# One decoder layer on one core: expert slots refilled in strict order, the router slot loaded after the count, and a product of the last norm given to GpSimd

## The chip, the cores and the metric

The kernel runs on one core of one Trainium2 chip. The core has five engines that each follow their own queue of instructions and meet only through semaphores: TensorE (PE, matrix products), VectorE (DVE), ScalarE (ACT), GpSimd (POOL) and SyncE (SP, which here issues nearly all transfers). A transfer is split over 16 DMA engines. The metric is the time of the whole program on the device in microseconds (us), the median of several runs.

## The reference

The reference is one layer of a hybrid decoder on 256 tokens of 1024 columns, in float32:

```
h = x + W_o(sum_i sigmoid(G_i xn) * P_i(mixer_i(xn))),  xn = RMSNorm(x)
h = h + HierMoE(RMSNorm(h))
out = RMSNorm(h)

HierMoE: g_sel = argmax(x @ wg + bg)            # 4 groups
         top_v, top_i = top_k(e_in, 2)          # 2 of the 8 experts of the group
         for e in range(32):
             hid = silu(x @ w1[e]) * (x @ w3[e])
             out = out + combine[:, e] * (hid @ w2[e])
RMSNorm(x) = x * rsqrt(mean(x*x) + 1e-6) * g
```

The first half has three mixers (sparse attention, pooling, a short convolution). The second half has 32 experts of width 256, and their weights are most of what is read from memory: about 100 MB of the 138 MB of the program.

## The kernel before

The first half (to about 207 us of the profile) computes the mixers and `W_o`. The second half routes the tokens and runs the experts in 8 blocks of 4 experts. Each expert takes up to 32 tokens (`CAP`) in a pass, so a block fills the 128 rows of TensorE.

**The ring.** Weights of the experts come in chunks of 1 MB (`ECHUNK`, 128 partitions x 2048 floats). A block has 12 chunks (`NQ`): 8 for the first product (w1 and w3) and 4 for the second (w2). SBUF has a ring of 25 slots of that size (`SLOTS`), in which the first half keeps its own tiles too. Four blocks, 48 chunks, make a round (`NC`); the table `AT` gives the slot of each chunk of a round. Chunks 0 to 24 take slots 0 to 24. From chunk 25 on the table says which slot is refilled: chunk 25 takes slot 0, chunk 26 takes slot 2, chunk 27 slot 3, and so on. SP issues the loads in the order of the chunks. Ahead of each it waits on `expert_used`, which TensorE raises once for each chunk that it has read; `earlier(c)` is the chunk that held the slot last. Chunks 25 to 29 are single loads (L631), the later ones pairs of 2 MB (L634, and L647 in the loop of SP that loads the second round).

**The router slot.** Slot 24 holds, in the first half and during the routing, small tiles of the router: constants (`conr`), the mask, and `pcnt`, in which VectorE works out how many passes are needed (`count_passes`, L1333 to L1337, ended by `passes_done`). Chunk 24 is loaded into that slot at L627.

**The start of the experts on TensorE.** TensorE counts the tokens of each expert with two small products of ones (L1772, `count_full`), gathers the tokens of the first block in four steps k (L1810, two products each), waits for `passes_done`, loads the number of passes into a register (L1816) and enters the loop of blocks, whose first product on chunk 0 is L1834. Between the first products stand the gathers of the next tokens (L1802).

**The end.** After the last block VectorE and ScalarE compute the last norm. VectorE copies a half row of the tokens 128 to 255 from PSUM (L1412), sums its squares (L1413), multiplies it by the norm's vector `fing` (`gain`, L1408, 512 columns), makes the next product of 256 columns (L1408), adds up the means (L1417, L1421); GpSimd raises them to the power -0.5 (L737); then VectorE scales the tokens 0 to 127 (L1425), ScalarE the others (L989), and the result is written out. `fin`, `fing`, `last_squares` and `act_squares` are laid over slots 12 to 15 of the ring, whose chunks have been used by then.

The order on each engine is that of the code; no scheduler moves anything.

Of the kernel before, what the change touches and what calls it, by code (L numbers as in the profile page):

```python
# [6 lines left out]
ALU = mybir.AluOpType  # L7
# [6 lines left out]
P = 128  # L14
# [28 lines left out]
EPS = 1e-6  # L43
NEG = -1e30
SLOT = 2048
SLOTS = 25
# [30 lines left out]

AT = [*range(SLOTS), 0, *range(2, SLOTS - 1)]
CHUNK_SET = {n: (SET_A, SET_B)[i % 2] for i, n in enumerate(SPLITS)}

NQ1 = KT
NQ2 = NQT
NQ = NQ1 + NQ2
ROUND = 4
NC = ROUND * NQ
# [25 lines left out]
K_ID = 0  # L113
K_IOTA = K_ID + P

K_TRI = K_IOTA + CAP
K_ONE = K_TRI + P
K_SL = K_ONE + P
K_RK = K_SL + HEADS
K_FOLD = K_RK + PER_GROUP  # L120
K_CAP = K_FOLD + 32
K_FOLD2 = K_CAP + MAXPASS
K_CB = K_FOLD2 + RC

# [10 lines left out]
def build(nc, x, params, consts, front, projs, small, wgrp, vecs, routerw, routerb, experts, out):  # L135
    with ExitStack() as ctx:
# [45 lines left out]
        wg = router("wg", [P, 2, P])  # L182
        pcnt = router("pcnt", [P, 8 + MAXPASS])
        hidT = sb("hidT", [P, 4, KVG, 32])
# [59 lines left out]
        comb, rank = routed[:, 0], routed[:, 1]  # L244
        mask = over("mask", [P, NT, NE], "ring", in_router[0] - 8 - MAXPASS - 2 * P)[:]


        fin = over("fin", [P, NT, D], "ring", 12 * SLOT)
        fing = over("fing", [P, D], "ring", 13 * SLOT)
        last_squares = over("last_squares", [P, NT, D], "ring", 14 * SLOT)  # L250
        act_squares = over("act_squares", [P, NT, D], "ring", 15 * SLOT)
        xgT = kv[:].rearrange("p (k s) -> p k s", k=KT)
# [10 lines left out]
        first, second_of, both = [gflat[:, i * NT * RC:(i + 1) * NT * RC] for i in range(3)]  # L263
        top1, big1, top2, big2, behind, e2, weight, c1, c2, total = [vflat[:, 256 + 16 * i:256 + 16 * i + NT * ROWS] for i in range(10)]
        gexp = vflat[:, 416:432].rearrange("p (t e) -> p t e", t=NT)
        share1, share2 = [vflat[:, i * NT * NE:(i + 1) * NT * NE].rearrange("p (t e) -> p t e", t=NT) for i in range(2)]
# [17 lines left out]
        fold2 = conr[:, K_FOLD2 - K_TRI:K_FOLD2 + RC - K_TRI]  # L284
        steps_of_cap = conr[:, K_CAP - K_TRI:K_CAP + MAXPASS - K_TRI]

# [118 lines left out]
        dve_fin = sem("dve_fin")  # L405
        act_fin = sem("act_fin")
        comb_done = sem("comb_done")
        comb_in = sem("comb_in")
# [93 lines left out]
        SCATTERED = (3, 5, 6, 7, 7)  # L502


        def summed(t, qt):
# [12 lines left out]
        def _(sp):  # L518
# [106 lines left out]
            early(SLOT_XHI, SLOT_ATT)  # L625
            sp.wait_ge(passes_done, 1)
            sp.dma_start(ring[:, SLOT_ROUTER], single(SLOT_ROUTER)).then_inc(router_slot_in, 16)  # L627

            for c in range(SLOTS, SLOTS + SINGLES):
                sp.wait_ge(expert_used, GIVEN + earlier(c) + 1)  # L630
                sp.dma_start(ring[:, AT[c]], single(c)).then_inc(expert_in[AT[c] // 2] if c % 2 else single_in, 16)  # L631
            for c in range(SLOTS + SINGLES, NC - 2, 2):
                sp.wait_ge(expert_used, GIVEN + earlier(c + 1) + 1)
                sp.dma_start(slots_of(c), experts[c // NQ, c % NQ // 2]).then_inc(expert_in[AT[c] // 2], 16)  # L634
            half = ECHUNK // 2
            for c, f, sem_in in ((NC - 2, slice(0, ECHUNK), expert_in[AT[NC - 2] // 2]), (NC - 1, slice(0, half), last_half_in),
                                 (NC - 1, slice(half, ECHUNK), last_in)):
                sp.wait_ge(expert_used, GIVEN + earlier(c) + 1)
                sp.dma_start(ring[:, AT[c], f], single(c)[:, f]).then_inc(sem_in, 16)
# [3 lines left out]
            with sp.Fori(1, passes * (NB // ROUND)) as r:  # L643
                def pair(c):

                    sp.wait_ge(expert_used, r * NC + (GIVEN + max(earlier(c), earlier(c + 1)) + 1))
                    sp.dma_start(slots_of(c), rounds[bass.ds(r % (NB // ROUND), 1), c // NQ, c % NQ // 2]  # L647
                                 .rearrange("o p c -> (o p) c")).then_inc(expert_in[AT[c] // 2], 16)

                for c in range(0, SLOT_ROUTER, 2):  # L650
                    pair(c)
                for c, sem_in in ((SLOT_ROUTER, router_slot_in), (SLOTS, expert_in[0])):
                    o = c % 2 * ECHUNK
                    sp.wait_ge(expert_used, r * NC + (GIVEN + earlier(c) + 1))
                    sp.dma_start(ring[:, AT[c]], rounds[bass.ds(r % (NB // ROUND), 1), c // NQ, c % NQ // 2, :, o:o + ECHUNK]
                                 .rearrange("o p c -> (o p) c")).then_inc(sem_in, 16)
                for c in range(SLOTS + 1, NC - 2, 2):
                    pair(c)
                for c, f, sem_in in ((NC - 2, slice(0, ECHUNK), expert_in[AT[NC - 2] // 2]), (NC - 1, slice(0, half), last_half_in),
                                     (NC - 1, slice(half, ECHUNK), last_in)):  # L660
                    sp.wait_ge(expert_used, r * NC + (GIVEN + earlier(c) + 1))
                    o = c % 2 * ECHUNK
                    sp.dma_start(ring[:, AT[c], f], rounds[bass.ds(r % (NB // ROUND), 1), c // NQ, c % NQ // 2, :, o + f.start:o + f.stop]
                                 .rearrange("o p c -> (o p) c")).then_inc(sem_in, 16)
# [9 lines left out]
        def _(pool):  # L674
# [58 lines left out]
            nc.gpsimd.tensor_tensor(flat(comb), flat(share1), flat(share2), ALU.add).then_inc(comb_ready, 1)  # L733

            for t in range(NT):
                pool.wait_ge(means_done, 2 + t)
# [3 lines left out]
        def _(act):  # L740
# [245 lines left out]
            for half in range(2):  # L986
                c = slice(half * 512, (half + 1) * 512)
                act.wait_ge(gained, (1, 3)[half])
                nc.scalar.activation(fin[:, 1, c], fin[:, 1, c], ACT.Copy, scale=stat[:, 31:32]).then_inc(act_fin, 1)  # L989
# [4 lines left out]
        def _(dve):  # L994
# [409 lines left out]
            def gain(p, c, sums, squares_done):  # L1404
# [6 lines left out]
            half_row = last_squares[:, 1, 512:D]  # L1411
            step(nc.vector.tensor_copy(half_row, bank[5][:]))  # L1412
            step(nc.vector.scalar_tensor_tensor(last_squares[:, 1, 0:512], half_row, 1.0 / D, half_row, ALU.mult, ALU.mult,  # L1413
                                                accum_out=stat[:, 13:14]))
            gain(1, slice(0, 512), half_row, 3 * NT)
            gain(2, slice(512, 768), summed(1, 2), 3 * NT + 3)
# [13 lines left out]
        def _(pe):  # L1430
# [354 lines left out]
            def have_expert(bb, j, q):  # L1785
# [8 lines left out]
                else:  # L1794
                    pe.wait_ge(expert_in[AT[c] // 2], bb * 32 + 16 * (turn(c) + 2))

# [10 lines left out]
            pe.wait_ge(sel_step, 1)  # L1807
            for k in range(4):
                for t in range(NT):
                    ins = mm(bank[2 + k // 2][:, (k % 2) * P:(k % 2 + 1) * P], h[:, t, k * P:(k + 1) * P],  # L1810
                             flat(sel[:, t]), start=(t == 0), stop=(t == NT - 1))
                if k % 2:
                    ins.then_inc(xg_full, 1)

            pe.wait_ge(passes_done, 1)
            passes = pe.value_load(npass[0:1, 0:1], min_val=1, max_val=MAXPASS)  # L1816

# [217 lines left out]
```

## Time and profile before

| | us |
|---|---|
| median of 3 runs | 416.36 |
| lowest and highest run | 415.26, 416.62 |
| the profiled execution | 415.54 |
| its span in the profile | 413.7 |

| engine | busy us | share of the span |
|---|---|---|
| TensorE | 382.1 | 92% |
| VectorE | 198.4 | 48% |
| ScalarE | 149.0 | 36% |
| GpSimd | 12.2 | 3% |

The time of an execution is 1.84 us above its span in the profile; what lies around the span is not in the trace. 139.89 MB move over the 16 DMA engines, at a mean of 338 GB/s over the span. In the page's 40 slices the DMA engines are 60% or less busy in most slices between 83 and 176 us, and 98% or more in nearly all from 207 us to 403 us. Times in the rows are counted from the start of the span.

### The profile page before, as it was taken

How to read it: one execution, taken by the hardware profiler on the slowest of the kernel's cores; microseconds unless marked ns; L12 is line 12 of the kernel's file. 1: busy time of each engine (PE TensorE's matmuls, PEld its weight loads, DVE VectorE, ACT ScalarE, POOL GpSimd, SP SyncE). 2: the span in 40 equal slices, each digit the busy share in tenths (PEclk: the TensorE clock that was granted, in tenths of full speed). 3: DMA queues.
4: the chain of work that ended last, by engine and by line, in shares of the span. 5: the costliest groups of instructions: out<-in, count | busy, mean ns of one | idle time of the engine just before them, and what ended most of it. 6: DMA issues, size and time to landing. Idle time of an engine off the chain costs nothing.

```text
span 413.7 us, 7503 instructions
## 1 busy us (share of the span) xinstructions
PE 382.1 (92%) x2990; PEld 265.2 (64%) x2990; DVE 198.4 (48%) x392; ACT 149.0 (36%) x283; POOL 12.2 (3%) x34
## 2 busy tenths in 40 slices
PE   7999999999999999999989999999899998688582
PEld 5999988767777777788865555555355544245241
DVE  3838693999898775784263121212122221211215
ACT  6834451638565635442221222222222222112023
POOL 3000000300000000000011000000000000000001
PEclk9999999999999999999999999999999999879996
DMA  7999999643441587569998999999999999999982
GB/s 299 412 412 358 395 390 365 265 152 101 154 147 67 196 329 281 184 243 398 420 418 321 394 428 429 426 414 430 426 425 428 426 417 429 428 428 428 425 335 103
DMA packets 17599, 139.89 MB, mean 338 GB/s; under 512 B 2336, under 2 KB 2720, under 8 KB 5792
## 3 DMA queue, kind: packets, MB, share of 16 engines
q1 hardware_dynamic: 16704, 138.60, 83.5%
q10 hardware_dynamic: 864, 0.84, 0.6%
q8 instruction: 24, 0.39, 0.4%
q14 instruction: 7, 0.06, 0.0%
HBM read 138.38 MB, written 1.05 MB: 337 GB/s over the span
## 4 chain that ended last, share of the span: by engine, by line
PE 73%; DMA 13%; DVE 6%; SPq 4%; ACT 2%; issue 2%; POOL 0%; POOLq 0%; DVEq 0%; ACTq 0%
DMA ring<-in_experts 12%; PE bank L1834 10%; PE bank L1802 6%; PE bank L1874 6%; PE bank L1596 5%; PE bank L1598 4%; PE bank L1597 4%; PE bank L1454 4%; PE bank L1455 4%; PE bank L1456 4%; SPq L647 4%; PE bank L1886 3%; PE bank L1718 2%; PE bank L1719 2%; PE bank L1717 2%
## 5 line engine op out<-in xcount | busy, mean ns | idle before, releaser
L1834 PE MATMUL bank<-ring,kv 128*32 128x512 f32 x512 | 65.7, 619 | 10.1 <-DMA ring<-in_experts 8.9
L481 DVE TENSOR_TENSOR part<-ring,part 128x2048 fp32r<-128x2048 f32 (+1 forms) x26 | 57.8, 2231 | 17.1 <-ACT part L474 17.1
L474 ACT CAST part<-ring 128x2048 fp32r<-128x2048 f32 (+1 forms) x26 | 48.0, 1847 | 29.5 <-DMA ring<-in_front 29.4
L1802 PEld LDWEIGHTS bank<-qcur,h 128*128 128x128 f32 x256 | 31.7, 191 | 28.2 <-issue 27.3
L1376 DVE SCALAR_TENSOR_TENSOR ylo<-bank,stat,yN 128x256 fp32r<-128x256 f32 (+1 forms) x40 | 17.1, 430 | 54.1 <-ACT yN L952 34.1
L1596 PE MATMUL bank<-part,xhi 128*128 128x512 f32 x96 | 39.2, 408 | 0.0
L1802 PE MATMUL bank<-qcur,h 128*128 128x128 f32 x256 | 39.1, 289 | 0.0
L1874 PE MATMUL bank<-ring,hidT 128*32 128x256 f32 (+1 forms) x640 | 35.2, 342 | 3.9 <-DMA ring<-in_experts 3.4
L1598 PE MATMUL bank<-part,xlo 128*128 128x512 f32 x96 | 37.6, 391 | 0.0
L1597 PE MATMUL bank<-part,xhi 128*128 128x512 f32 x96 | 37.5, 391 | 0.0
L1454 PE MATMUL bank<-xhi,part 128*128 128x256 f32 x128 | 36.6, 286 | 0.5 <-DVE xlo L1021 0.5
L1455 PE MATMUL bank<-xlo,part 128*128 128x256 f32 x128 | 36.2, 283 | 0.0
L1456 PE MATMUL bank<-xhi,part 128*128 128x256 f32 x128 | 36.2, 283 | 0.0
L1834 PEld LDWEIGHTS bank<-ring,kv 128*32 128x32 f32 x512 | 13.0, 110 | 32.0 <-issue 23.6
L952 ACT ACTIVATE yN<-bank,stat 128x256 fp32r<-128x256 f32 (+1 forms) x40 | 17.2, 431 | 42.3 <-PE bank L1874 42.3
L944 ACT ACT_TABLE_LOAD x7 | 9.0, 1283 | 50.6 <-DVE stat L1366 50.6
L1886 PE MATMUL bank<-yN,cmbT 128*128 128x256 f32 (+1 forms) x80 | 23.4, 318 | 2.8 <-DVE ylo L1376 2.5
L1454 PEld LDWEIGHTS bank<-xhi,part 128*128 128x128 f32 x128 | 24.5, 192 | 1.7 <-DVE xlo L1021 0.9
L1874 PEld LDWEIGHTS bank<-ring,hidT 128*32 128x32 f32 x640 | 16.6, 109 | 13.6 <-ACT hidT L946 3.1
L1455 PEld LDWEIGHTS bank<-xlo,part 128*128 128x128 f32 x128 | 24.6, 192 | 0.0
L1456 PEld LDWEIGHTS bank<-xhi,part 128*128 128x128 f32 x128 | 24.6, 192 | 0.0
L1360 DVE TENSOR_TENSOR kv<-bank,prm 128x512 f32<-128x512 f32 x8 | 5.5, 692 | 39.7 <-PE bank L1802 39.7
(251 smaller groups left out, 586.9 us busy)
## 6 DMA issues: line engine op xcount, KB each, us to landing
ring<-in_experts SPq DMA_DIRECT2D x30, 2048.0 KB, 33.5
ring<-in_experts SPq DMA_DIRECT2D x34, 1024.0 KB, 8.4
ring<-in_front SPq DMA_DIRECT2D x28, 1024.0 KB, 5.4
ring<-in_front SPq DMA_DIRECT2D x4, 512.0 KB, 6.8
ring<-in_projs SPq DMA_DIRECT2D x4, 512.0 KB, 5.2
ring<-in_experts SPq DMA_DIRECT2D x4, 512.0 KB, 32.5
ring<-in_front SPq DMA_DIRECT2D x2, 560.0 KB, 9.4
h<-in_x SPq DMA_DIRECT2D x2, 512.0 KB, 3.8
```

The lines of the kernel that those rows point to most:

```text
L474: nc.scalar.copy(high(n, half)[:, 0:c].bitcast(F32R), raw(n, half)[:, 0:c]).then_inc(hi_done, 1)
L481: nc.vector.tensor_tensor(low(n, half)[:, 0:c].bitcast(F32R), raw(n, half)[:, 0:c], high(n, half)[:, 0:c], ALU.subtract).then_inc(split_do ...
L1454: mm(dst, whi, ahi, start=start, stop=False)
L1455: mm(dst, whi, alo, start=False, stop=False)
L1456: return mm(dst, wlo, ahi, start=False, stop=stop)
L1596: mm(bank[t][:], XH[:, kk, cols], whi[:, k], start=(kk == 0), stop=False)
L1597: mm(bank[t][:], XH[:, kk, cols], wlo[:, k], start=False, stop=False)
L1598: ins = mm(bank[t][:], XL[:, kk, cols], whi[:, k], start=False, stop=(kk == KT - 1))
L1802: ins = mm(bank[2][:, (k % 4) * P:(k % 4 + 1) * P], h[:, t, k * P:(k + 1) * P], flat(sel[:, t]), start=(t == 0), stop=(t == NT - 1))
L1834: ins = mm(bank[0][CAP * e:CAP * (e + 1)], xgT[:, q, CAP * e:CAP * (e + 1)], expert(j, q, e), start=(q == 0), stop=(q == NQ1 - 1))
L1874: ins = mm(second_out(p, slice(CAP * e, CAP * (e + 1))), hT[:, ht, CAP * e:CAP * (e + 1)], second_weights(j, p, ht, e), start=(ht == 0), s ...
L1886: mm(sum_of_piece(t, p), onehot, yN[:, place(p)].bitcast(F32R), start=False, stop=False)
```

## The change

1. `AT` becomes `[0..24, 0, 1, 2, ..., 22]`: chunk 26 takes slot 1, chunk 27 slot 2, and so on to chunk 47 in slot 22. So each chunk from 26 on waits for the use of a chunk that is one earlier in the order. The semaphore of arrival is no longer chosen by the slot but by `c % 24 // 2`, so that pairs keep one semaphore.
2. The vector of the steps of `CAP` moves from `conr` (in the router slot) to `con`, and `pcnt` from the router slot to a part of `vbd`. The load of chunk 24 waits for `count_full` in place of `passes_done`.
3. TensorE waits for `passes_done` and loads the number of passes ahead of the last of the four gather steps, not behind it.
4. The tiles of the last norm move down by one slot (11 to 14).
5. GpSimd makes the product of the half row with `fing` (512 columns) as soon as VectorE has copied the half row (`half_copied`), and VectorE no longer makes it. ScalarE waits for `half_gained` there. On GpSimd the product stands ahead of the powers.

```diff
-AT = [*range(SLOTS), 0, *range(2, SLOTS - 1)]
+AT = [*range(SLOTS), *range(ROUND * NQ - SLOTS)]
...
-        pcnt = router("pcnt", [P, 8 + MAXPASS])
...
+        pcnt = vflat[:, 432:440 + MAXPASS]
...
-        steps_of_cap = conr[:, K_CAP - K_TRI:K_CAP + MAXPASS - K_TRI]
+        steps_of_cap = con[:, K_CAP:K_CAP + MAXPASS]
...
+        def arrival(c):
+
+            return expert_in[c % SLOT_ROUTER // 2]
...
-            sp.wait_ge(passes_done, 1)
+            sp.wait_ge(count_full, 1)
             sp.dma_start(ring[:, SLOT_ROUTER], single(SLOT_ROUTER)).then_inc(router_slot_in, 16)
...
+            pool.wait_ge(vec_in, 16)
+            pool.wait_ge(half_copied, 1)
+            nc.gpsimd.tensor_tensor(fin[:, 1, 0:512], last_squares[:, 1, 512:D], fing[:, 0:512], ALU.mult).then_inc(half_gained, 1)
             for t in range(NT):
                 pool.wait_ge(means_done, 2 + t)
...
-                act.wait_ge(gained, (1, 3)[half])
+                act.wait_ge(*((half_gained, 1), (gained, 2))[half])
...
-            step(nc.vector.tensor_copy(half_row, bank[5][:]))
+            nc.vector.tensor_copy(half_row, bank[5][:]).then_inc(half_copied, 1)
+            dve.wait_ge(half_copied, 1)
             step(nc.vector.scalar_tensor_tensor(last_squares[:, 1, 0:512], half_row, 1.0 / D, half_row, ALU.mult, ALU.mult,
                                                 accum_out=stat[:, 13:14]))
-            gain(1, slice(0, 512), half_row, 3 * NT)
             gain(2, slice(512, 768), summed(1, 2), 3 * NT + 3)
...
             for k in range(4):
+                if k == 3:
+                    pe.wait_ge(passes_done, 1)
+                    passes = pe.value_load(npass[0:1, 0:1], min_val=1, max_val=MAXPASS)
                 for t in range(NT):
                     ins = mm(bank[2 + k // 2][:, (k % 2) * P:(k % 2 + 1) * P], h[:, t, k * P:(k + 1) * P],
                              flat(sel[:, t]), start=(t == 0), stop=(t == NT - 1))
                 if k % 2:
                     ins.then_inc(xg_full, 1)
-
-            pe.wait_ge(passes_done, 1)
-            passes = pe.value_load(npass[0:1, 0:1], min_val=1, max_val=MAXPASS)
```

TensorE at the start of the experts: `qcur` holds the selection of tokens, `npass` the number of passes, `kv` the gathered tokens. Before:

```order
L1772 MATMUL bank<-mask,conr 128x32 x2
L1810 MATMUL bank<-qcur,h 128x128 [waits sel_step]
L1810 MATMUL bank<-qcur,h 128x128 x7
L1816 TENSOR_LOAD npass [waits passes_done]
L1816 ISA x2
L1909 UNCONDITIONAL_BRANCH
L1909 ISA
L1795 ISA [waits xg0_done,hn_done]
L1834 MATMUL bank<-ring,kv 32x512 [waits expert_in0]
```

and now:

```order
L1782 MATMUL bank<-mask,conr 128x32 x2
L1823 MATMUL bank<-qcur,h 128x128 [waits sel_step]
L1823 MATMUL bank<-qcur,h 128x128 x5
L1821 TENSOR_LOAD npass [waits passes_done]
L1821 ISA x2
L1823 MATMUL bank<-qcur,h 128x128 x2
L1919 UNCONDITIONAL_BRANCH
L1919 ISA
L1805 ISA [waits xg0_done,hn_done]
L1844 MATMUL bank<-ring,kv 32x512 [waits expert_in0]
```

The load of the register has moved ahead of the last two products of the gather.

VectorE at the last norm, before:

```order
L1412 COPY last_squares<-bank 128x512 [waits comb_done]
L1413 SCALAR_TENSOR_TENSOR last_squares,stat<-last_squares 128x512 [waits dve_step]
L1408 TENSOR_TENSOR fin<-last_squares,fing 128x512 [waits ssq_done,comb_done,dve_step]
L1406 REGISTER_ALU
L1408 TENSOR_TENSOR fin<-bank,fing 128x256 [waits ssq_done,comb_done]
L1417 SCALAR_TENSOR_TENSOR stat<-stat 128x2
L1421 TENSOR_TENSOR stat<-stat 128x1 [waits ssq_done,means_done]
```

and now:

```order
L1422 COPY last_squares<-bank 128x512 [waits comb_done]
L1424 SCALAR_TENSOR_TENSOR last_squares,stat<-last_squares 128x512 [waits half_copied]
L1416 REGISTER_ALU [waits dve_step]
L1418 TENSOR_TENSOR fin<-bank,fing 128x256 [waits ssq_done,comb_done]
L1427 SCALAR_TENSOR_TENSOR stat<-stat 128x2
L1431 TENSOR_TENSOR stat<-stat 128x1 [waits ssq_done,means_done]
```

The product of 512 columns is gone from VectorE. GpSimd at the same place has it now, between the shares of the router and the powers of the means:

```order
L740 TENSOR_TENSOR routed<-vbd 128x64 [waits pool_step]
L744 TENSOR_TENSOR fin<-last_squares,fing 128x512 [waits half_copied,vec_in]
L747 TENSOR_TENSOR stat<-stat 128x1 [waits means_done] x2
L136 UNCONDITIONAL_BRANCH
```

Ahead of the change its last rows were L733 and the two of L737.

## Rows read from the trace of the kernel before

**Rows 1.** Late part of the chain of work: start, length, what it was.

```profile
348.27 49.81 DMA ring<-in_experts
```

**Rows 2.** Windows: stretch, length, engines' busy us (instructions), PEclk, DMA share, GB/s.

```profile
218.00:221.00 3.00, 2.70 (x24) 1.67 (x23) 0.98 (x4) 0.62 (x2) 0.32 (x1) 1.00 0.88 279
...
218.60:218.80 0.20, 0.20 (x4) 0.20 (x2) 0.00 (x0) 0.17 (x1) 0.00 (x0) 1.00 0.31 123
...
224.00:227.00 3.00, 3.00 (x34) 1.32 (x30) 1.85 (x6) 0.81 (x1) 0.00 (x0) 1.00 0.76 246
...
229.00:232.00 3.00, 2.87 (x27) 1.82 (x23) 0.48 (x1) 0.84 (x2) 0.00 (x0) 1.00 0.87 336
218.00:240.00 22.00, 21.25 (x214) 11.82 (x212) 5.88 (x16) 5.74 (x14) 0.32 (x1) 1.00 0.95 365
240.00:398.00 158.00, 140.69 (x1331) 73.38 (x1330) 32.29 (x80) 32.92 (x75) 0.00 (x0) 0.98 1.01 425
360.00:375.00 15.00, 11.85 (x105) 5.25 (x100) 1.46 (x4) 2.27 (x5) 0.00 (x0) 0.79 1.00 424
398.00:405.74 7.74, 7.08 (x100) 4.92 (x100) 3.00 (x7) 3.67 (x11) 0.00 (x0) 1.00 0.48 193
```

**Rows 3.** Timeline of SP, the loads of chunks 24, 25 and 26: start, length.

```profile
218.03 0.33 SPq L627 DMA_DIRECT2D ring<-in_experts  x1
220.43 0.33 SPq L631 DMA_DIRECT2D ring<-in_experts  x1
...
224.60 0.33 SPq L631 DMA_DIRECT2D ring<-in_experts  x1
```

**Rows 4.** Timeline of PE, the gather and the products on chunks 0 and 1.

```profile
216.95 2.05 PE L1810 MATMUL bank<-qcur,h 128*128 128x128 f32 x16
...
219.31 1.07 PE L1834 MATMUL bank<-ring,kv 128*32 128x512 f32 x8 [0.30 <-issue]
...
221.39 1.06 PE L1834 MATMUL bank<-ring,kv 128*32 128x512 f32 x8
```

**Rows 5.** PE's sequencer at L1816: duration ns min/median/max, first and last start.

```profile
L1816 PEldq TENSOR_LOAD <-npass x1: 490/490/490, 218.0 to 218.0; - x1
```

**Rows 6.** Timeline of DVE: the first step of the count of passes.

```profile
216.93 0.19 DVE L1333 TENSOR_REDUCE pcnt<-bank 128x1 f32<-128x32 f32 x1
```

**Rows 7.** Timeline of the last norm.

```profile
405.44 0.69 DVE L1413 SCALAR_TENSOR_TENSOR last_squares<-last_squares 128x512 f32<-128x512 f32 x1
...
406.17 0.69 DVE L1408 TENSOR_TENSOR fin<-last_squares,fing 128x512 f32<-128x512 f32 x1
...
406.78 0.42 DVE L1408 TENSOR_TENSOR fin<-bank,fing 128x256 f32<-128x256 f32 x1
407.12 0.15 DVE L1417 SCALAR_TENSOR_TENSOR stat<-stat 128x2 f32<-128x2 f32 x1
...
407.54 1.07 POOL L737 TENSOR_TENSOR stat<-stat 128x1 f32<-128x1 f32 x2 [189.16 <-DVE stat L1421]
...
408.64 1.34 ACT L989 ACTIVATE fin<-fin,stat 128x512 f32<-128x512 f32 x2 [2.02 <-POOL stat L737]
```

**Rows 8.** Timeline of products of GpSimd, and of VectorE beside them.

```profile
30.18 1.07 POOL L713 TENSOR_TENSOR rw<-rw,prm 128x512 f32<-128x512 f32 x1 [22.23 <-DMA rb<-in_routerb]
...
73.55 1.41 DVE L1118 TENSOR_SCALAR att<-att,coef 128x128 f32<-128x128 f32 x1
73.59 1.30 POOL L718 TENSOR_TENSOR mixlo<-mixed,mixhi 128x512 fp32r<-128x512 f32 x1
...
80.64 1.29 POOL L718 TENSOR_TENSOR mixlo<-mixed,mixhi 128x512 fp32r<-128x512 f32 x1
...
80.97 0.60 DVE L1104 SCALAR_TENSOR_TENSOR att<-conf,conr,bank 128x384 f32<-128x384 f32 x1
```

**Rows 9.** Two lines of DVE: duration ns min/median/max, first and last start.

```profile
L1118 DVE TENSOR_SCALAR att<-att,coef x16: 285/286/1410, 73.6 to 140.5; 128x128 f32<-128x128 f32 x16
...
L1117 DVE TENSOR_TENSOR coef<-coef,gts x16: 160/161/466, 73.1 to 140.3; 128x2 f32<-128x2 f32 x16
```

More of the change, by code:

```diff
@@ L44 @@
 NEG = -1e30
+NQ1 = KT
+NQ2 = NQT
+NQ = NQ1 + NQ2
+ROUND = 4
 SLOT = 2048
@@ L76 @@
 SLOT_ATT, SLOT_Q, SLOT_ROUTER = 22, 23, 24
-AT = [*range(SLOTS), 0, *range(2, SLOTS - 1)]
+AT = [*range(SLOTS), *range(ROUND * NQ - SLOTS)]
 CHUNK_SET = {n: (SET_A, SET_B)[i % 2] for i, n in enumerate(SPLITS)}
[L83 to L86, printed above, removed]
 NC = ROUND * NQ
@@ L114 @@
 K_IOTA = K_ID + P
-K_TRI = K_IOTA + CAP
+K_CAP = K_IOTA + CAP
+K_TRI = K_CAP + T // CAP
 K_ONE = K_TRI + P
@@ L120 @@
 K_FOLD = K_RK + PER_GROUP
-K_CAP = K_FOLD + 32
-K_FOLD2 = K_CAP + MAXPASS
+K_FOLD2 = K_FOLD + 32
 K_CB = K_FOLD2 + RC
@@ L244, in build @@
         comb, rank = routed[:, 0], routed[:, 1]
[L245 to L251, printed above, removed]
+        mask = over("mask", [P, NT, NE], "ring", in_router[0] - 2 * P)[:]
+        fin = over("fin", [P, NT, D], "ring", 11 * SLOT)
+        fing = over("fing", [P, D], "ring", 12 * SLOT)
+        last_squares = over("last_squares", [P, NT, D], "ring", 13 * SLOT)
+        act_squares = over("act_squares", [P, NT, D], "ring", 14 * SLOT)
         xgT = kv[:].rearrange("p (k s) -> p k s", k=KT)
@@ L406, in build @@
         act_fin = sem("act_fin")
+        half_copied = sem("half_copied")
+        half_gained = sem("half_gained")
         comb_done = sem("comb_done")
@@ L630, in _ @@
                 sp.wait_ge(expert_used, GIVEN + earlier(c) + 1)
-                sp.dma_start(ring[:, AT[c]], single(c)).then_inc(expert_in[AT[c] // 2] if c % 2 else single_in, 16)
+                sp.dma_start(ring[:, AT[c]], single(c)).then_inc(arrival(c) if c % 2 else single_in, 16)
             for c in range(SLOTS + SINGLES, NC - 2, 2):
                 sp.wait_ge(expert_used, GIVEN + earlier(c + 1) + 1)
-                sp.dma_start(slots_of(c), experts[c // NQ, c % NQ // 2]).then_inc(expert_in[AT[c] // 2], 16)
+                sp.dma_start(slots_of(c), experts[c // NQ, c % NQ // 2]).then_inc(arrival(c), 16)
             half = ECHUNK // 2
-            for c, f, sem_in in ((NC - 2, slice(0, ECHUNK), expert_in[AT[NC - 2] // 2]), (NC - 1, slice(0, half), last_half_in),
+            for c, f, sem_in in ((NC - 2, slice(0, ECHUNK), arrival(NC - 2)), (NC - 1, slice(0, half), last_half_in),
                                  (NC - 1, slice(half, ECHUNK), last_in)):
@@ L647, in pair @@
                     sp.dma_start(slots_of(c), rounds[bass.ds(r % (NB // ROUND), 1), c // NQ, c % NQ // 2]
-                                 .rearrange("o p c -> (o p) c")).then_inc(expert_in[AT[c] // 2], 16)
+                                 .rearrange("o p c -> (o p) c")).then_inc(arrival(c), 16)
                 for c in range(0, SLOT_ROUTER, 2):
                     pair(c)
-                for c, sem_in in ((SLOT_ROUTER, router_slot_in), (SLOTS, expert_in[0])):
+                for c, sem_in in ((SLOT_ROUTER, router_slot_in), (SLOTS, arrival(SLOTS))):
                     o = c % 2 * ECHUNK
@@ L658, in _ @@
                     pair(c)
-                for c, f, sem_in in ((NC - 2, slice(0, ECHUNK), expert_in[AT[NC - 2] // 2]), (NC - 1, slice(0, half), last_half_in),
+                for c, f, sem_in in ((NC - 2, slice(0, ECHUNK), arrival(NC - 2)), (NC - 1, slice(0, half), last_half_in),
                                      (NC - 1, slice(half, ECHUNK), last_in)):
@@ L1794, in have_expert @@
                 else:
-                    pe.wait_ge(expert_in[AT[c] // 2], bb * 32 + 16 * (turn(c) + 2))
+                    pe.wait_ge(arrival(c), bb * 32 + 16 * (turn(c) + 2))
             def gather(*ks):
```

## The prediction, made before any run

> **What bounds the kernel now.** I read the chain of work first, for what ends last. Its late part is one entry: a load of the ring that was issued at 348.27 and landed 49.81 us later [rows 1]. A load of 2 MB that takes 50 us to land stands in a queue, so the next view is the table of windows, for whether that queue is ever empty. From 240 to 398 us the DMA engines are busy all the time (share 1.01) at 425 GB/s, with no gap [rows 2]. So from 240 us on the end is set by bytes: the last chunk lands when all chunks ahead of it have moved, and no faster engine changes that.
>
> The bytes do not move at that rate in the 22 us ahead. From 218 to 240 us the mean is 365 GB/s [rows 2]. Against 425 that is 60 GB/s x 22 us = 1320 KB, or 3.1 us of transfer time. The windows show three holes: 218 to 221 at 279 GB/s (146 x 3 = 438 KB, 1.03 us), 224 to 227 at 246 (179 x 3 = 537 KB, 1.26 us), 229 to 232 at 336 (89 x 3 = 267 KB, 0.63 us); small shortfalls and surpluses make up the rest. As the queue never runs dry later, each us taken out of these holes brings the last chunk forward by one us. This is the most that the refills can give: 3.1 us.
>
> Whose fault are they? The timeline of SP says: chunk 24 is issued at 218.03, chunk 25 at 220.43, chunk 26 at 224.60 [rows 3]. The first hole is that of chunk 24: SP has nothing in flight any more when it may issue. The second is that of chunk 26, which waits until chunk 2 has been read.
>
> What follows the last chunk is a fixed tail of some 15 us, the second products, the combination, the last norm, and the write.
>
> **Part 1, the slots in order.** Today chunk 26 is issued behind the use of chunk 2, at 224.60. With the new table it waits for chunk 1, whose product ends at 221.39 + 1.06 = 222.45 [rows 4], so it is issued at about 222.5, 2.1 us sooner. What a late issue costs I take from the two holes themselves. The flow is down to 123 GB/s from 218.6 on [rows 2], 0.57 us behind the issue of chunk 24, and the first hole costs 1.03 us: so an issue needs about 0.57 + 1.03, some 1.5 us, before its bytes make up for an empty queue. The second hole agrees: chunk 25's bytes end at about 224.6, the issue at 224.60 plus 1.5 would cost 1.5, and 1.26 was seen. So a load costs max(0, issue + 1.5 - end of the bytes ahead). For chunk 26 that becomes 222.5 + 1.5 = 224.0 against about 224.6: nothing. The chunks behind it are each one use sooner too, some 1.7 to 2 us, and the second hole goes: -1.26 us at its site.
>
> **Part 2, chunk 24 behind the count.** The count of tokens is ready when VectorE starts on it at 216.93 [rows 6], at the latest; the number of passes only at 218.0 [rows 5]. SP issues chunk 24 at about 216.95 in place of 218.03. 216.95 + 1.5 = 218.45 is ahead of 218.6, so the first hole goes: -1.03 us at its site.
>
> **But a hole comes back between them.** Chunk 25 refills slot 0 in both versions, and waits for the use of chunk 0, which neither part moves forward. Chunk 24's 1 MB takes 1048 KB / 425 = 2.47 us, so its bytes now end at 218.6 + 2.5 = 221.1. Chunk 25 is issued at 220.43 plus the 0.15 us of part 3: 220.6 + 1.5 = 222.1, 1.0 us too late. So of 2.29 us in two holes 1.0 us returns in one, and 1.25 to 1.3 us are gained. The third hole, 0.63 us, has no cause that I can read: chunks 27 to 29 were in the queue by then. If it was a thin queue it goes too, if not it stays. Ends for the stream: a gain of 1.25 - 0.3 (the 1.5 us is rough) = 0.95 and of 1.25 + 0.63 + 0.2 = 2.1 us. I take the middle of the two cases of the third hole, 1.5 us.
>
> [...]
>
> **Part 3, the register load on TensorE.** The load starts at 218.0 and takes 0.49 us [rows 5]; the sequencer is then ahead of the array, which is still busy with the gather of 2.05 us from 216.95 [rows 4]. With the load ahead of the last step, its two products (four of the 16 instructions, 4 x 0.13 = 0.5 us) can be handed out only after about 218.8, where the array today has them behind it at 219.0. They then end at about 219.3 to 219.4, and the first product on chunk 0, today at 219.31, starts at 219.4 to 219.5. Bounds: 0 (they fit beside the branch) and 0.5 us (all of it in series); I take 0.15. Queued behind it on TensorE is everything of the experts, but only the first refills feel it, and it is in the sum above. The other consumers of the gather (VectorE's scaling of the last two steps) have until chunk 2's product at about 223.5: nothing.
>
> **Part 4, tiles of the norm one slot lower, constants in another tile.** The vector `fing` is loaded behind the same use as before, and 8 more columns in a small early load lie under the first half: nothing.
>
> **Part 5, the product on GpSimd.** Today VectorE makes the squares from 405.44 (0.69 us), the 512-column product from 406.17 (0.69), the 256-column one from 406.78, and starts on the means at 407.12; the powers start on GpSimd at 407.54, and ScalarE scales from 408.64, after which the write ends the program [rows 7]. Were that all, taking out the product would bring the means, the powers and the end forward by 406.78 - 406.17 = 0.61 us. GpSimd's product would run from 405.5 for 1.07 to 1.30 us [rows 8], done by 406.8, under the powers' 406.93.
>
> Against it stand the rows of products on GpSimd earlier. VectorE's L1118 takes 0.285 us at best, and 1.41 when it starts at 73.55 with GpSimd's product at 73.59: it ends as that product does, at 74.9 [rows 8, 9]. L1117, two elements wide with two operands in SBUF, takes 0.16 and once 0.47, at 73.1, where GpSimd was busy with the copy ahead of that product [rows 9]. But L1104, with one of its tensors in PSUM, takes 0.60 us inside GpSimd's product of 1.29 us at 80.64, and is not drawn out [rows 8]. So a VectorE instruction of the first kinds and a GpSimd product do not overlap, the later one waits. The squares (two operands in SBUF) are of that kind, the 256-column product (PSUM and SBUF) is not, the means L1417 (two operands in SBUF) are. `half_copied` frees both engines at once. Which is first no row tells; I take VectorE, as the signal is its own. Then GpSimd waits until 406.1, runs 1.07 to 1.30 us to 407.2 to 407.4, the 256-column product passes beside it, and L1417 stands until it is over: 407.2 to 407.4 in place of 407.12. Cost +0.05 to +0.3 us; I take +0.2, nearest to the row with two full operands (1.30).
>
> The Trainium skill ("SBUF — State Buffer", SBUF: two separate sides) has this as a rule that speaks against the change: VectorE and GpSimd share one pair of ports under an exclusive lock, and "whichever starts first gets the pair for the whole instruction", for VectorE with two SBUF inputs against a GpSimd operation that reads SBUF. By that rule part 5 costs 0.2 and without it it gives 0.6; the rows of L1117 and L1118 agree with it.
>
> **The sum.** Stream -1.5, norm +0.2: -1.3 us. The profiled execution took 415.54 (span 413.7 and 1.84 around it), so 414.2 of that kind; it lies 0.8 under the median of the runs, which is noise of the same size as the change. Against the median of 416.36 the forecast is 415.06, said as 415.1.
>
> **Rivals.**
> - *The hole only moves.* If the new hole before chunk 25 is as large as the old two, for instance because part 3 costs 0.5 us and the ramp of a load is nearer 2 us (1.26 + 1.03 - 1.85), the stream gains some 0.4 us and the norm takes 0.2: 416.2. For it: chunk 25's issue is the one that neither part moves. Against it: the ramp seen twice is 1.3 to 1.6 us.
> - *No exclusion at the end.* GpSimd's product runs beside the squares, the norm gives 0.6: -2.1 us, 414.3. Against it the rows of L1117.
> - *GpSimd first.* Its product runs 405.5 to 406.8, the squares behind it, everything 0.7 us later: -0.8, 415.6. It needs GpSimd to start ahead of VectorE's own signal.
> - *A lower clock in the tail (slower than before).* TensorE's granted clock has a mean of 0.79 from 360 to 375 us, where it is busy 11.85 of 15 us between waits for weights, while the tail from 398 has 1.00 with 7.08 us of busy TensorE [rows 2]. The change moves these waits by 1.5 us. If a low stretch (1.2 in place of 2.4 GHz) fell on the tail for its whole length, it would cost up to 7 us, for half of it 3.5: 416.36 - 1.3 + 3.5 = 418.6. It decides from a low stretch of 1.3 us / 0.5, 2.6 us in the tail, on. Against it: the pattern of waits moves as a whole.
> - *It doesn't do what it says.* The order shows it does; only that chunk 24 was held by something other than the number of passes could spoil part 2, and SP's issue 0.03 us after the load of that number began rules it out.
>
> **Chances.** Forecast, a net gain of 0.75 to 1.9 us: 0.60. The hole moves: 0.16. No exclusion: 0.08. GpSimd first: 0.10. Lower clock: 0.06. A measurement of this kernel tells about 0.3%, 1.25 us, from no change. In the forecast's case a good half lies beyond that (0.38 of 0.60), in that of no exclusion all, in that of GpSimd first a fifth: faster 0.48; slower by over 0.3% is the lower clock, 0.06; within 0.3% the rest, 0.46. The range from 414.0 to 416.4 leaves out the lower clock, a stream gain with all three holes closed, and little else.
>
> **What would show it.** SP's load of chunk 24 at about 217.0 and of chunk 26 about 2 us sooner; windows from 218 to 240 us at some 390 to 400 GB/s in place of 365, with one hole at about 221 to 223; the last block's waits about 1.5 us sooner. At the end GpSimd's product recorded with 1.7 to 2 us (its wait in it) or VectorE's squares with more than 0.69 us, and the means recorded with 0.5 to 0.9 us. Wrong if the refills are sooner and the last chunk is not, if the 218-to-240 mean stays at 365, or if the time from the squares to the powers shortens by 0.6 us.

## The result

| | us | runs |
|---|---|---|
| before | 415.67 median (415.24 to 416.62) | 5 |
| changed | 413.10 median (412.58 to 414.15) | 5 |
| ratio | 0.9940, 95% interval 0.9924 to 0.9955 | |

The change makes the kernel 2.5 us faster (1.9 to 3.2 by the interval), about twice the 1.3 us that was forecast, and its median lies below the range (414.0 to 416.4). The kernel before came out at 415.67 with five runs, 0.7 us under the 416.36 that the forecast was taken from; that is 0.7 of the 2.0 us between 415.1 and 413.10, and the size of the gain is the rest. A second set of five runs gave 412.75 us against 415.56 (ratio 0.9929, 0.9912 to 0.9947). The profiled execution has a span of 411.2 us against 413.7.

The windows of the changed kernel, with the columns of [rows 2]: stretch, length, busy us of PE, PEld, DVE, ACT and POOL, granted clock, DMA share, GB/s.

```profile
218.00:221.00 3.00, 2.65 (x21) 1.51 (x20) 1.14 (x4) 0.62 (x2) 0.46 (x2) 1.00 1.04 399
221.00:224.00 3.00, 3.00 (x28) 1.92 (x30) 0.02 (x1) 0.00 (x0) 0.00 (x0) 1.00 0.79 254
224.00:227.00 3.00, 3.00 (x30) 1.25 (x30) 1.84 (x6) 0.41 (x1) 0.00 (x0) 1.00 0.99 382
227.00:229.00 2.00, 2.00 (x24) 0.55 (x20) 0.40 (x1) 0.88 (x1) 0.00 (x0) 1.00 0.96 311
229.00:232.00 3.00, 2.88 (x26) 1.79 (x18) 0.48 (x1) 0.74 (x2) 0.00 (x0) 1.00 0.98 410
218.00:240.00 22.00, 21.21 (x212) 11.67 (x210) 6.04 (x16) 5.35 (x13) 0.46 (x2) 1.00 0.98 385
...
240.00:390.00 150.00, 137.46 (x1306) 73.17 (x1306) 31.80 (x79) 32.48 (x75) 0.00 (x0) 0.98 1.01 429
```

The same last stretch of the kernel before:

```profile
240.00:390.00 150.00, 135.20 (x1293) 71.14 (x1292) 31.81 (x79) 32.07 (x73) 0.00 (x0) 0.98 1.01 425
```

The first six lines are what was forecast: the holes at 218 and 224 us of [rows 2] are gone or nearly so (399 and 382 GB/s), one has come back at 221, and the mean from 218 to 240 is 385 GB/s in place of 365: 20 x 22 = 440 KB, 1.0 us. The last line is what was not: for 150 us in which the queue is never empty in either kernel, the stream runs at 429 GB/s in place of 425. That is 4 x 150 = 600 KB, another 1.4 us. Together 2.4 of the 2.5 us. TensorE starts its first product on the last chunk at 395.44 in place of 398.21 and VectorE the last squares at 402.67 in place of 405.44, both 2.77 us sooner. From the powers to the end of the span it is 6.4 us in place of 6.2, but over all traces of this case that stretch takes 6.0 to 6.6, so the difference tells nothing.

The loads of SP in the changed kernel, chunks 24, 25 and 26 (the second row groups chunks 25 and 26), and the row of chunk 26 by itself:

```profile
217.08 0.33 SPq L634 DMA_DIRECT2D ring<-in_experts  x1
220.83 2.41 SPq L638 DMA_DIRECT2D ring<-in_experts  x2
```

```profile
222.92 0.33 SPq L638 DMA_DIRECT2D ring<-in_experts  x1
```

Chunk 24 goes out 0.95 us sooner than in [rows 3], chunk 26 1.68 us sooner, chunk 25 0.40 us later. On TensorE the gather is now cut in two, and the first product on chunk 0 starts later than in [rows 4]:

```profile
217.12 1.61 PE L1823 MATMUL bank<-qcur,h 128*128 128x128 f32 x12
219.07 0.71 PE L1823 MATMUL bank<-qcur,h 128*128 128x128 f32 x4 [0.34 <-issue]
219.71 1.06 PE L1844 MATMUL bank<-ring,kv 128*32 128x512 f32 x8
```

The last norm, to be laid beside [rows 7]:

```profile
401.95 0.69 DVE L1422 COPY last_squares<-bank 128x512 f32<-128x512 f32 x1
...
402.67 0.69 DVE L1424 SCALAR_TENSOR_TENSOR last_squares<-last_squares 128x512 f32<-128x512 f32 x1
...
402.78 1.70 POOL L744 TENSOR_TENSOR fin<-last_squares,fing 128x512 f32<-128x512 f32 x1 [184.24 <-DVE last_squares L1422]
...
403.56 0.42 DVE L1418 TENSOR_TENSOR fin<-bank,fing 128x256 f32<-128x256 f32 x1 [0.19 <-ACT act_squares L982]
...
403.91 0.60 DVE L1427 SCALAR_TENSOR_TENSOR stat<-stat 128x2 f32<-128x2 f32 x1
404.54 0.23 DVE L1431 TENSOR_TENSOR stat<-stat 128x1 f32<-128x1 f32 x2
...
404.78 1.07 POOL L747 TENSOR_TENSOR stat<-stat 128x1 f32<-128x1 f32 x2 [0.29 <-DVE stat L1431]
```

VectorE starts its squares first, GpSimd's product 0.11 us behind it; that product is recorded with 1.70 us and ends at 404.48, and the means on two elements (L1427), which took 0.15 us in the kernel before, are recorded with 0.60 and end just behind it, at 404.51. From the start of the squares to the powers it is 2.11 us, against 407.54 - 405.44 = 2.10 in [rows 7]. The product has left VectorE and nothing has moved.

The granted clock of this last stretch, the eighth column, is 1.00, as it was before:

```profile
396.00:403.70 7.70, 6.53 (x96) 4.45 (x87) 3.53 (x9) 4.36 (x15) 0.92 (x1) 1.00 0.39 157
```

### The profile page after: what moved, and what is told of

It is laid out like the page before. It is cut to its first block, busy times and chain, and to the rows that moved or that the text cites. A ratio compares the mean times of both kernels' runs of the same rounds, so it can differ in the third digit from the quotient of the medians.

```text
span 411.2 us, 7504 instructions
## 1 busy us (share of the span) xinstructions
PE 381.5 (93%) x2990; PEld 265.6 (65%) x2990; DVE 198.6 (48%) x391; ACT 148.9 (36%) x283; POOL 13.8 (3%) x35
## 4 chain that ended last, share of the span: by engine, by line
PE 73%; DMA 13%; DVE 6%; SPq 3%; ACT 2%; issue 1%; POOL 0%; POOLq 0%; DVEq 0%; ACTq 0%
DMA ring<-in_experts 12%; PE bank L1844 10%; PE bank L1812 6%; PE bank L1884 6%; PE bank L1606 5%; PE bank L1607 4%; PE bank L1608 4%; PE bank L1464 4%; PE bank L1465 4%; PE bank L1466 4%; SPq L654 3%; PE bank L1896 3%; PE bank L1727 2%; PE bank L1728 2%; PE bank L1729 2%; PE bank L1568 1%
## 5 line engine op out<-in xcount | busy, mean ns | idle before, releaser
L1812 PEld LDWEIGHTS bank<-qcur,h 128*128 128x128 f32 x256 | 32.8, 196 | 28.4 <-issue 27.6
L1812 PE MATMUL bank<-qcur,h 128*128 128x128 f32 x256 | 40.1, 295 | 0.0
L1896 PEld LDWEIGHTS bank<-yN,cmbT 128*128 128x128 f32 x80 | 15.0, 188 | 13.9 <-DVE ylo L1386 11.1
```

The source lines that it names most:

```text
L1812: ins = mm(bank[2][:, (k % 4) * P:(k % 4 + 1) * P], h[:, t, k * P:(k + 1) * P], flat(sel[:, t]), start=(t == 0), stop=(t == NT - 1))
L1896: mm(sum_of_piece(t, p), onehot, yN[:, place(p)].bitcast(F32R), start=False, stop=False)
```

## The experiments

Each has five to eleven runs, made beside runs of the kernel before on the same chip. The ratio is to those runs. Their median is 415.56 us for the lines from "changed, again" to "refills one use late"; 415.79 for "ring moved 32 bytes", "ring as before", "norm's product on VectorE" and "register load behind"; and 415.71 for the other four. "Rate" is that of one trace of each, from 240 to 390 us. Up to 240 us the changed kernel, its second set, the one with the norm's product on VectorE and the one with the squares' factor from PSUM give TensorE, SP and the DMA engines the same instructions; their 218-to-240 column reads 385, 385, 376 and 384. So a difference below some 9 GB/s there (0.5 us) tells nothing from one trace.

| kernel | median us | ratio to before, 95% interval | 218 to 240 us, GB/s | rate, GB/s |
|---|---|---|---|---|
| before | 415.67 | | 365 | 425 |
| changed | 413.10 | 0.9940 (0.9924 to 0.9955) | 385 | 429 |
| changed, again | 412.75 | 0.9929 (0.9912 to 0.9947) | 385 | 429 |
| slots in order only | 412.95 | 0.9935 (0.9917 to 0.9954) | 385 | 429 |
| early chunk 24 only | 414.01 | 0.9963 (0.9950 to 0.9975) | 359 | 429 |
| refills one use late | 414.55 | 0.9976 (0.9963 to 0.9989) | 349 | 429 |
| before, ring moved 32 bytes | 414.12 | 0.9953 (0.9934 to 0.9971) | 360 | 429 |
| changed, ring as before | 414.41 | 0.9969 (0.9956 to 0.9981) | 384 | 425 |
| changed, ring at 128 | 414.19 | 0.9963 (0.9950 to 0.9976) | 381 | 426 |
| norm's product on VectorE | 413.04 | 0.9930 (0.9911 to 0.9948) | 376 | 429 |
| register load behind | 413.17 | 0.9934 (0.9915 to 0.9953) | 388 | 429 |
| squares' factor from PSUM | 412.86 | 0.9935 (0.9920 to 0.9949) | 384 | 429 |
| refill of slot 0 in halves | 413.28 | 0.9943 (0.9930 to 0.9955) | 382 | 429 |
| last three together | 412.47 | 0.9928 (0.9915 to 0.9941) | 389 | 429 |

**The parts one by one.** The first question was whether the higher rate is an accident of one execution or belongs to a part.

The changed kernel again:

> The changed kernel once more, beside the three parts. Theory A (all of the gain lies in the two holes of the transfers at 218 to 227 us, and the execution profiled of it had besides a lucky rate later on): about 1.3 us below the kernel before, and a mean of 425 GB/s from 240 to 390 us as before. Theory B (something in the change raises the rate of the whole stream): 2.5 us below, and 428 GB/s again.

Only the table of slots (against the changed kernel the edits are these, and the norm's product is back in VectorE's `gain`):

```diff
-            sp.wait_ge(count_full, 1)
+            sp.wait_ge(passes_done, 1)
             sp.dma_start(ring[:, SLOT_ROUTER], single(SLOT_ROUTER)).then_inc(router_slot_in, 16)
...
-            nc.gpsimd.tensor_tensor(fin[:, 1, 0:512], last_squares[:, 1, 512:D], fing[:, 0:512], ALU.mult).then_inc(half_gained, 1)
...
-                if k == 3:
-                    pe.wait_ge(passes_done, 1)
-                    passes = pe.value_load(npass[0:1, 0:1], min_val=1, max_val=MAXPASS)
```

> Only the table of slots in order (with the tiles of the norm one slot lower); chunk 24 waits for the number of passes, the register load stands behind the gather, and VectorE makes the product of the last norm. A: the hole ahead of chunk 26 goes, that of chunk 24 stays: -1.2 us. B, if the table of slots is what raises the rate: -2.3 us or more, with 428 GB/s from 240 to 390 us.

Only chunk 24 behind the count (slots, semaphores of arrival, norm and register load as before):

```diff
-            sp.wait_ge(passes_done, 1)
+            sp.wait_ge(count_full, 1)
             sp.dma_start(ring[:, SLOT_ROUTER], single(SLOT_ROUTER)).then_inc(router_slot_in, 16)
```

> Only chunk 24 behind the count (with the count of passes in the other tile); slots, register load and norm as before. The first hole goes, but chunk 25 and chunk 26 come no sooner, so the transfers only reach the hole ahead of chunk 25 and 26 earlier: both theories expect -0.3 us or less, 0 within the noise.

The changed kernel with each refill from chunk 26 on one use later, in each of SP's waits:

```diff
-                sp.wait_ge(expert_used, GIVEN + earlier(c) + 1)
+                sp.wait_ge(expert_used, GIVEN + earlier(c) + 1 + (c > SLOTS))
```

> The changed kernel, but each refill from chunk 26 on waits for one use more than its slot needs, as it did in the kernel before; the places in the ring are the new ones. A: the hole ahead of chunk 26 is back, 1.2 us slower than the changed kernel. B with the places as the cause: only 1.2 us slower, still 1.2 below before, at 428 GB/s. B with the deeper queue as the cause: all but the first hole lost, back at the time of before within 0.5 us, at 425 GB/s.

The rate repeats (429 again), so it is no accident, and theory A falls. But theory B, as first put, falls too: the kernel with the old slots and that with the late refills have 429 as well. The early load of chunk 24, which moves fewer bytes from 218 to 240 us than the kernel before (359 GB/s against 365), is 1.55 us faster than it (0.9963, 0.9950 to 0.9975). Here are its windows and those of the slots-only and the late kernel, in this order:

```profile
218.00:240.00 22.00, 21.24 (x213) 11.81 (x211) 6.06 (x16) 5.56 (x13) 0.49 (x2) 1.00 0.95 359
```

```profile
218.00:240.00 22.00, 21.19 (x213) 11.77 (x212) 6.02 (x16) 5.57 (x14) 0.43 (x2) 1.00 0.98 385
```

```profile
218.00:240.00 22.00, 21.31 (x212) 11.77 (x210) 6.07 (x17) 5.23 (x12) 0.59 (x3) 1.00 0.92 349
```

Two things follow. The refills in order do bring the bytes forward (385 GB/s, with or without the early chunk 24), and the early chunk 24 alone shows no gain (359). And something that all four kernels share, and the kernel before has not, sets the rate. Besides a few semaphores there is one such thing: the tile of constants `con` is 8 floats wider, and the ring, allocated behind it, starts 32 bytes higher in each partition. It starts at byte 9440 of each partition before (224 above a multiple of 256) and at 9472 = 37 x 256 after.

**The place of the ring.** The kernel before with 32 unused bytes ahead of the ring (the few tiles allocated behind the ring move with it):

```diff
+        sb("pad", [P, 8])
         ring = sb("ring", [P, SLOTS, SLOT])
```

> The kernel before with an unused tile of 32 bytes a partition ahead of the ring, and nothing else. The ring starts at byte 9440 of a partition in the kernel before (224 above a multiple of 256) and at 9472 (a multiple of 256) in the changed one and in all four kernels measured so far, because the tile of constants ahead of it grew by 32 bytes. Theory C (the place of the ring in memory sets the rate of the stream): 429 GB/s from 240 to 390 us in place of 425, and 1.4 us below before. Theory D (the kernel before was profiled in a poor execution, and the rest comes from the refills): 425 to 429 GB/s by chance and a time within 0.4 us of before.

The changed kernel with the ring at 9696, 224 above a multiple of 256 as before:

```diff
+        stat = sb("stat", [P, 44])
+        npass = sb("npass", [P, 2], I32)
         ring = sb("ring", [P, SLOTS, SLOT])
-        stat = sb("stat", [P, 44])
...
-        npass = sb("npass", [P, 2], I32)
```

> The changed kernel with two small tiles (stat, npass) allocated ahead of the ring, not behind it, so that the ring starts 224 bytes above a multiple of 256, as in the kernel before. Theory C: 425 GB/s from 240 to 390 us, 1.4 us slower than the changed kernel, 1.2 to 1.4 us below before. Theory D: as the changed kernel, 2.6 to 2.8 us below before.

The changed kernel with the ring at 8832, 128 above a multiple of 256:

```diff
-        con = sb("con", [P, K_TRI])
...
+        npass = sb("npass", [P, 2], I32)
         ring = sb("ring", [P, SLOTS, SLOT])
+        con = sb("con", [P, K_TRI])
```

> The changed kernel with npass ahead of the ring and the constants behind it, so that the ring starts 128 bytes above a multiple of 256. If only a start on a multiple of 256 bytes gives the higher rate: 425 GB/s from 240 to 390 us and 1.4 us slower than the changed kernel. If a multiple of 64 or 128 is enough: 429 GB/s and the time of the changed kernel.

Windows of the three, in this order:

```profile
240.00:390.00 150.00, 137.25 (x1292) 72.44 (x1292) 31.83 (x79) 32.30 (x74) 0.00 (x0) 0.97 1.01 429
```

```profile
240.00:390.00 150.00, 136.19 (x1298) 72.10 (x1301) 31.83 (x79) 32.42 (x75) 0.00 (x0) 0.98 1.01 425
```

```profile
240.00:390.00 150.00, 136.10 (x1306) 72.16 (x1306) 31.80 (x79) 32.47 (x75) 0.00 (x0) 0.99 1.01 426
```

Theory C holds both ways. With 32 bytes the kernel before gains 1.67 us (1.2 to 2.7 by the interval of the ratio), with every instruction as it was. The changed kernel with the ring off the multiple of 256 loses 1.2 to 1.4 us: it is 1.38 below its kernel before, where the changed kernel is 2.57 and 2.81 below. A start on a multiple of 128 is not enough: 426 GB/s and 414.19 us. The DMA share is 1.01 in all of them, so the engines are no less busy, each byte takes them longer. The tiles behind the ring change their places in these three kernels too, and no run moves the ring alone; but in all of them, and in the kernels before and changed, every load issued from 240 to 390 us goes into the ring, except one of 0.5 MB into `fing`, which lies in the ring's slots.

The second of the three is also the changed kernel as the prediction had it in mind, with its stream at 425 GB/s. It is 1.38 us faster than the kernel before (0.9969, 0.9956 to 0.9981), and 1.3 was forecast.

With the ring's place out of the way the parts are read against the kernel before with its ring moved (1.67 us below its kernel before, 360 GB/s from 218 to 240 us). The early chunk 24 is 1.55 below its own: nothing, and 359 GB/s. The slots in order are 2.61 below: 0.9 us more, and 385 GB/s. All of the change is 2.57 to 2.81 below: 0.9 to 1.1 more. Each of these differences is uncertain by some 0.8 us or more, as the intervals of the ratios show, so they agree with the 25 GB/s x 22 us = 550 KB, 1.3 us, of the windows and don't fix the size.

**The product of the norm.** The changed kernel with the product on VectorE again:

```diff
-            nc.gpsimd.tensor_tensor(fin[:, 1, 0:512], last_squares[:, 1, 512:D], fing[:, 0:512], ALU.mult).then_inc(half_gained, 1)
...
-                act.wait_ge(*((half_gained, 1), (gained, 2))[half])
+                act.wait_ge(gained, (1, 3)[half])
...
+            gain(1, slice(0, 512), half_row, 3 * NT)
             gain(2, slice(512, 768), summed(1, 2), 3 * NT + 3)
```

> The changed kernel with the product of the last norm back on VectorE. If the exclusion between the engines costs what the prediction said, 0.2 us below the changed kernel; by the trace of the changed kernel (2.83 us from the copy to the powers in both) the same time within 0.1 us; if the product on GpSimd gained anything, slower by up to 0.6 us.

413.04 us, no difference, as the trace of the changed kernel said. Does the product gain nothing because the two engines exclude each other? Then a VectorE instruction with only one operand in SBUF should let GpSimd through:

```diff
-            step(nc.vector.scalar_tensor_tensor(last_squares[:, 1, 0:512], half_row, 1.0 / D, half_row, ALU.mult, ALU.mult,
+            step(nc.vector.scalar_tensor_tensor(last_squares[:, 1, 0:512], bank[5][:], 1.0 / D, half_row, ALU.mult, ALU.mult,
```

> The changed kernel with VectorE's squares of the half row reading one of the two factors from PSUM, not both from the copy in SBUF. If two operands in SBUF are what makes VectorE and GpSimd exclude each other: GpSimd's product is recorded with 1.1 to 1.3 us in place of 1.70 and the means start 0.4 us sooner behind the copy, 0.3 to 0.45 us below the changed kernel. If they exclude each other for another reason, no difference.

Its timeline of the last norm:

```profile
402.30 0.69 DVE L1422 COPY last_squares<-bank 128x512 f32<-128x512 f32 x1
...
403.14 1.27 POOL L744 TENSOR_TENSOR fin<-last_squares,fing 128x512 f32<-128x512 f32 x1 [184.53 <-DVE last_squares L1422]
...
404.26 0.16 DVE L1427 SCALAR_TENSOR_TENSOR stat<-stat 128x2 f32<-128x2 f32 x1
...
404.69 1.07 POOL L747 TENSOR_TENSOR stat<-stat 128x1 f32<-128x1 f32 x2 [0.29 <-DVE stat L1431]
```

The product takes 1.27 us in place of 1.70, the means 0.16 in place of 0.60, and from the copy to the powers it is 2.39 us in place of 2.83. The last run below, with the same edit, has the same 1.27 us and 2.39 us. So the second operand in SBUF is what made GpSimd wait. The 0.44 us are in the traces; the time (412.86) does not tell them from nothing.

**The register load and the hole at 221 us.** The register load behind the gather again:

```diff
             for k in range(4):
-                if k == 3:
-                    pe.wait_ge(passes_done, 1)
-                    passes = pe.value_load(npass[0:1, 0:1], min_val=1, max_val=MAXPASS)
...
+            pe.wait_ge(passes_done, 1)
+            passes = pe.value_load(npass[0:1, 0:1], min_val=1, max_val=MAXPASS)
```

> The changed kernel with TensorE's wait and register load behind the gather again. The first product on chunk 0 should start at 219.45 in place of 219.71, chunk 25 be issued 0.25 us sooner, and the whole be 0.25 us below the changed kernel; if chunk 25's issue doesn't set the hole at 221 us, the same time.

```profile
219.51 1.06 PE L1844 MATMUL bank<-ring,kv 128*32 128x512 f32 x8 [0.30 <-issue]
```

The first product starts 0.20 us sooner than with the load in the gather (219.71), SP issues chunk 25 at 220.63 in place of 220.83, and the flow from 218 to 240 us (388 GB/s against 385) and the time (413.17) are the same within the noise. Counted from the start of the gather (217.16 here, 217.12 in the changed kernel) the load costs 2.59 - 2.35 = 0.24 us.

The refill of slot 0 in halves (TensorE raises `half_used` at the product of the second expert on chunk 0):

```diff
+            sp.wait_ge(half_used, 1)
+            sp.dma_start(ring[:, AT[SLOTS], 0:SLOT // 2], single(SLOTS)[:, 0:SLOT // 2]).then_inc(half_refilled, 16)
+            sp.wait_ge(expert_used, GIVEN + earlier(SLOTS) + 1)
+            sp.dma_start(ring[:, AT[SLOTS], SLOT // 2:], single(SLOTS)[:, SLOT // 2:]).then_inc(arrival(SLOTS), 16)
```

> The changed kernel with the refill of slot 0 (chunk 25) in two halves, the first of them issued when two of the four experts of chunk 0 have been used. If the hole at 221 to 223 us is set by the issue of chunk 25: its first half is issued 0.5 us sooner, the hole is smaller by 100 to 200 KB, 0.2 to 0.5 us below the changed kernel. Otherwise the same time.

```profile
220.83 0.33 SPq L639 DMA_DIRECT2D ring<-in_experts  x1
221.21 0.43 SPq L641 DMA_DIRECT2D ring<-in_experts  x1
```

The first half was issued no sooner than the whole chunk in the changed kernel (220.83), and the second 0.38 us later. So the experiment does not test what it was made for; 413.28 us says only that halves cost nothing that can be measured. Why the signal came no sooner can be read from the same trace: the 16 records of products on chunks 0 and 1 (eight for the four experts of each) take 0.604 us each on the average and all lie in 2.1 us, so about four are under way at a time. The four experts of a chunk seem to be computed side by side, the second ending with the fourth, and then an expert's use gives no earlier signal than the chunk's. That is read from modelled ends and from the late signal, and no run tests it. The 0.38 us between the halves is SP's own: its issue takes 0.33 us.

All three together (squares' factor from PSUM, halves, register load behind):

> The changed kernel with the squares' factor from PSUM, the refill of slot 0 in halves and the register load behind the gather again: the gains of the three together, 0.6 to 1.1 us below the changed kernel if all hold, the same time if none does.

412.47 us, the lowest median of all, but its interval against the kernel before overlaps that of the changed kernel. It is a version that is not worse, not one shown to be better.

## Why the prediction was right in its mechanism and wrong in its size

- **What bounds the kernel.** Right: the stream of weights. The first product on the last chunk is 2.77 us sooner, and so are the last squares. The granted clock of the last stretch is 1.00 as before, so the rival of a lower clock did not come.
- **Parts 1 and 2, and the hole between them.** Right in place and nearly in size. Chunk 24 at 217.08 (about 217.0 was said), chunk 26 at 222.92 (222.5), a hole at 221 to 224 with 254 GB/s: (425 - 254) x 3 = 513 KB, 1.2 us, where 1.0 was said. 385 GB/s were reached where 390 to 400 were expected, a gain of 1.0 us where the sum had 1.25 to 1.5. The third hole did not go, it came 2 us sooner: 227 to 229 us at 311 GB/s, (425 - 311) x 2 = 228 KB, 0.54 us, for the 0.63 at 229; its share of 0.3 us in the forecast was not there, and its cause stays open. And the single runs bear out what the prediction's formula implied and did not say: the early chunk 24 alone gains nothing that can be measured, since the hole ahead of chunk 25 takes its place.
- **Part 3.** Right: 0.15 us was taken, 0.24 is what the two traces show from the start of the gather to the first product on chunk 0. The other 0.17 us of its delay stand already in the start of the gather (217.12 against 216.95). They seem to come with the new places of the tiles: the kernel before with its ring moved has the gather at 217.10, in one trace.
- **Part 4.** This is the step that failed. The prediction costed the constants in another tile at "nothing", by the small load that fills it. It did not follow the allocation: 32 bytes more ahead of the ring put it on a multiple of 256, and the 64 MB of weights that pass into it from 240 to 390 us move at 429 GB/s in place of 425. That is -1.4 us from 240 us on by the traces, -1.67 us of time in the run that adds the 32 bytes and changes no instruction. The order of the instructions on the engines shows nothing of it, and the diff shows it only to someone who adds up the tiles.
- **Part 5.** Right in its mechanism: VectorE first, GpSimd drawn out to 1.70 us (1.7 to 2 was said), the means recorded with 0.60 (0.5 to 0.9 was said). The term was +0.2 and is 0.0: the product itself takes about 1.1 us once it runs (404.48 less some 403.3), nearer to the lower of the two rows it was weighed by (1.07 and 1.30). Neither of the two rivals came true: GpSimd did not go first, and its product did not run beside the squares.
- **The sum.** -1.5 and +0.2 were forecast; -1.0, 0.0 and the -1.4 of the ring's place were measured. Without the ring's move the change gives -1.38, so the -1.3 was right for what the prediction looked at; some of that is luck, since the windows give -1.0 of it (a stream gain 0.5 too large less a norm cost 0.2 too large) and the interval of that run is 0.8 to 1.8. The range ended at 414.0, since no bound in it stood for a rate of the stream other than 425. That rate was read from one kernel, and was taken as what the memory gives.

The Trainium skill ("DMA: Bandwidth & Descriptors", How a descriptor splits into AXI transactions) says of reads that a descriptor (one contiguous piece of a transfer) that doesn't start on a multiple of 256 bytes begins with a transaction from the boundary below. The packets of 8 KB or more that move from 240 to 390 us in the kernel before have some 15.6 KB each (about 63 MB in 4021), so most are rows of two slots, 16384 bytes. If writes into SBUF did the same, such a row would take 65 transactions and not 64, 1.6% more, an estimate from what the Trainium skill states; the runs show 0.9% at 224 bytes above the boundary and 0.7% at 128. So the runs agree with the boundary (256 and not 128) and not with the size, and what happens inside a DMA engine is left open.

The Trainium skill ("SBUF — State Buffer", SBUF: two separate sides) says that a VectorE instruction with two inputs in SBUF and a GpSimd operation that reads SBUF share a pair of ports, and that the one that starts first holds it for its whole length. The run that took one of VectorE's operands from PSUM agrees with it: GpSimd's product got shorter by 0.43 us (1.70 to 1.27).

## What to carry to other kernels

Where a stream of transfers sets the end, look at the start address of the tiles that it fills, and not only at when they come free: here 32 unused bytes gave 1.7 us of 416, no less than the reordering of the refills (0.9 to 1.4). When a diff changes the size of any tile, add up what is allocated behind it. Closing a gap in a stream of refills is worth only what the next refill's own wait leaves of it, and a product given to an idle engine gained nothing here, where its partner needed SBUF at that moment.

## What the runs showed of the hardware that was not expected

- Loads of 1 to 2 MB into a ring whose slots (8192 bytes a partition) start on multiples of 256 bytes: 429 GB/s in each of eleven traces, over 150 us with the queue never empty. At 224 above such a multiple 425 in two traces, at 128 above 426 in one. The DMA share is 1.01 in all.
- A GpSimd product of 128x512 that starts 0.11 us behind a VectorE instruction with two operands in SBUF is recorded with 1.70 to 1.71 us (seven traces), and with 1.27 us behind one with one operand in SBUF and one in PSUM (two traces). A VectorE instruction of two elements with two operands in SBUF, started while the product drawn out to 1.70 us still ran, is recorded until its end: 0.60 us in place of 0.15.
- TensorE's load of a register (0.49 us), placed inside a row of small products, left the array idle for 0.34 us and the following product 0.24 us later.
